# The last LayerNorm's weight and bias are read from PSUM by VectorE

## The reference, cut to what matters

```python
def _layernorm(x, w, b):
    xf = x.astype(jnp.float32)
    mu = jnp.mean(xf, axis=-1, keepdims=True)
    xc = xf - mu
    var = jnp.mean(xc * xc, axis=-1, keepdims=True)
    return (xc * lax.rsqrt(var + LN_EPS) * w.astype(jnp.float32) + b.astype(jnp.float32)).astype(x.dtype)
...
        moe = _hier_moe(h1, ...)
        ple = jax.nn.sigmoid(h1 @ w_ple_gate[i] + b_ple_gate[i]) * (p[i] @ w_ple[i])
        h = _layernorm(DN_ALPHA * h1 + moe + ple, ln2_w[i], ln2_b[i])
```

## Time and profile before

| what | value |
|---|---|
| median of 3 runs | 893.3 us (891.83 to 893.46) |
| the profiled execution's own time | 893.97 us |
| its span, first to last instruction | 892.2 us |
| mean granted TensorE clock | 0.966 |
| busy share of the span: PE, DVE, ACT, POOL | 87%, 49%, 20%, 18% |

### The profile page before, as it was taken

The page is one execution under the profiler, slowest core; times in us unless marked ns, Lnnn a source line. Parts: engine busy times, 40 slices in busy tenths (PEclk is TensorE's granted clock), DMA queues, the critical chain, the costliest instruction groups (busy, mean ns, idle before and its releaser), DMA issues.

```text
span 892.2 us, 9829 instructions
## 1 busy us (share of the span) xinstructions
PE 778.1 (87%) x3913; PEld 527.0 (59%) x3913; DVE 436.9 (49%) x743; ACT 179.4 (20%) x333; POOL 156.1 (18%) x74
## 2 busy tenths in 40 slices
PE   0399997799999999999999999999999989988700
PEld 0388786789887888544444688885554544544200
DVE  5999806455668888311135678362212220211138
ACT  4212323344232321000000110121111111111022
POOL 5734663220042221100000060000000000000042
PEclk9999998899999999999999999999999999999955
DMA  9523321111121132622110351807999999999562
GB/s 294 191 93 96 94 94 48 48 49 48 48 95 48 48 82 61 239 91 79 63 47 1 139 239 47 327 4 279 423 424 422 423 422 421 423 423 422 228 212 95
DMA packets 57860, 163.48 MB, mean 183 GB/s; under 512 B 14412, under 2 KB 37078, under 8 KB 45014
## 3 DMA queue, kind: packets, MB, share of 16 engines
q1 hardware_dynamic: 51744, 139.68, 41.2%
q0 software_dynamic: 3072, 12.63, 4.0%
q10 hardware_dynamic: 2998, 10.53, 2.9%
HBM read 148.15 MB, written 14.68 MB: 182 GB/s over the span
## 4 chain that ended last, share of the span: by engine, by line
PE 71%; DMA 15%; DVE 9%; issue 2%; ACT 1%; POOL 1%; SPq 1%; ACTq 0%; DVEq 0%; POOLq 0%
PE psum L744 24%; DMA ring<-in_w_exp_up_dram 11%; PE psum L1038 9%; PE psum L953 6%; PE psum L943 6%; PE psum L992 5%; PE psum L1053 3%; PE psum L934 3%; PE psum L1015 2%; DMA ring<-in_w_in_dram 2%; PE psum L1016 2%; DVE arena L1398 2%; PE psum L883 2%; DVE arena L1397 2%; PE psum L903 1%
## 5 line engine op out<-in xcount | busy, mean ns | idle before, releaser
L744 PE MATMUL psum<-ring_r 128*128 128x512 f32 (+1 forms) x768 | 213.3, 363 | 2.6 <-DVE arena L1569 1.3
L744 PEld LDWEIGHTS psum<-ring_r 128*128 128x128 f32 x768 | 139.4, 194 | 26.2 <-issue 2.4
L675 POOL TENSOR_TENSOR ring_r<-ring,ring_r 128x2048 fp32r<-128x2048 f32 x20 | 93.4, 4670 | 205.5 <-ACT ring_r L1109 205.5
L1038 PE MATMUL psum<-ring,arena 128*64 128x512 f32 x512 | 113.1, 594 | 11.5 <-DMA ring<-in_w_exp_up_dram 10.7
L1109 ACT COPY arena<-psum 128x512 f32<-128x512 f32 (+3 forms) x102 | 57.5, 582 | 290.8 <-PE psum L960 139.8
L744 PE MATMUL psum<-arena_r,ring_r 128*128 128x512 f32 x256 | 100.5, 392 | 0.0
L1038 PEld LDWEIGHTS psum<-ring,arena 128*64 128x64 f32 x512 | 40.2, 137 | 82.7 <-issue 81.8
L1824 DVE SCALAR_TENSOR_TENSOR arena<-arena,psum 128x256 f32<-128x256 f32 x16 | 9.9, 621 | 120.5 <-ACT arena L1291 120.5
L707 POOL DMA_INDIRECT ring<-y_rows,rowsU x8 | 9.1, 1132 | 328.5 <-ACT arena L1109 326.4
L1015 PE MATMUL psum<-arena_r 128*128 128x256 f32 x256 | 65.3, 293 | 0.0
L1016 PE MATMUL psum<-arena_r 128*128 128x256 f32 x256 | 62.5, 282 | 0.0
(11 more groups left out here) (242 smaller groups left out, 956.8 us busy)
## 6 DMA issues: line engine op xcount, KB each, us to landing
ring<-in_w_exp_gate_dram SPq DMA_DIRECT2D x32, 1024.0 KB, 17.3
ring<-in_w_exp_up_dram SPq DMA_DIRECT2D x32, 1024.0 KB, 19.5
ring<-in_w_exp_down_dram SPq DMA_DIRECT2D x32, 1024.0 KB, 19.4
ring<-in_w_in_dram SPq DMA_DIRECT2D x18, 1024.0 KB, 5.1
y_rows<-arena ACTq DMA_DIRECT2D x16, 512.0 KB, 8.0
y_rows<-arena POOLq DMA_DIRECT2D x4, 1024.0 KB, 7.2
ring<-in_w_out_ssd_dram SPq DMA_DIRECT2D x4, 1024.0 KB, 7.3
ring<-in_w_out_dram SPq DMA_DIRECT2D x4, 1024.0 KB, 11.1
```

The source lines that it names most:

```text
L675: g.tensor_tensor(lo, ring[:, SLOT_OF[seq]], hi.bitcast(F32), ALU.subtract).then_inc(s_w_lo, 1)
L744: t = mm(o, a, b, start=(first and j == 0), stop=(last and j == 2))
L1038: t = mm(psum[sides[half], parity, :], xgT[buf][:, k, c:c + CAP], ring[:, s:s + 2, k, :], start=(k == 0), stop=(k == KD - 1))
```

## The change

PE gets a step behind its overflow loop. It waits for `ln2_in` and then issues four matrix products. Each has as its stationary side one row of 128 ones, and as its moving side 512 columns of row 0 of `A1w` or `A1b`; the product is that piece of the row in all 128 partitions. The weight comes to stand in PSUM banks 0 and 1, the bias in banks 2 and 3, and a new semaphore `pe_ln2` tells that the four are done. DVE waits for `pe_ln2` in the place where it waited for `ln2_in`, and passes the two PSUM views to `tiles_normed`. POOL's tile 3 still reads `A1w` and `A1b` in SBUF. The first LayerNorm is as it was.

```diff
+        s_pe_ln2 = sem("pe_ln2")
...
                     down(j + PAIRS, j + PAIRS // 2, 0)
                 pe.nop()
+            pe.wait_ge(s_ln2_in, 32)
+            for j, row in enumerate((A1w, A1b)):
+                for b in range(2):
+                    t = mm(psum[:, 2 * j + b, :], ones[0:1, :], row[0:1, 512 * b:512 * b + 512], start=True, stop=True)
+            t.then_inc(s_pe_ln2, 1)
...
             dve.wait_ge(s_act_stats, 1 + NT - 1)
-            dve.wait_ge(s_ln2_in, 32)
-            tiles_normed(base, A1w, A1b, s_fin_ready)
+            dve.wait_ge(s_pe_ln2, 1)
+            w2, b2 = (psum[:, 2 * j:2 * j + 2, :].rearrange("p b n -> p (b n)") for j in range(2))
+            tiles_normed(base, w2, b2, s_fin_ready)
```

## The result

| | median us | lowest to highest | runs |
|---|---|---|---|
| kernel before, in this comparison | 892.11 | 891.48 to 893.46 | 5 |
| changed kernel | 888.15 | 886.34 to 888.97 | 5 |

The ratio is 0.9947, with a 95% interval of 0.9931 to 0.9964: the change makes the kernel 0.4 to 0.7% faster. The medians lie 3.96 us apart. The gain of 3.92 us that the forecast rests on agrees with the difference of the medians and lies inside the interval (3.2 to 6.2 us). The profiled execution took 888.41 us, with a span of 886.7.

The account below looks back on a forecast made before the run. The tail was taken as DVE's six norm steps plus 3.1 us, with PE busiest but unaffected. Tile 1's waits gave -3.92 us, other terms 0; from the median 893.3 that made 889.4 us, range 888.2 to 891.5.

Parts of the forecast that it names:

- the base of the sum: Whole kernel: the starting time for the forecast, the median 893.3 us, from which the gain was taken.
- The waits inside tile 1's steps: Final norm, DVE: tile 1's two steps stop waiting for POOL, 3.24 to 1.28 us each, -3.92 us.
- A PSUM input costs nothing: Final norm, DVE's six steps: reading the second input from PSUM adds 0 us.
- The far end: Final norm: PSUM slow as second input, 2.49 us a step, 896.6 us in all; rival's chance 3%.
- The open point, the second input from PSUM instead of the first: Tile 1's norm steps: input order might matter and free nothing, time staying at 893.3 us; rival's chance 7%.
- POOL at 2.2 us a step: Tile 3's norm: POOL's two steps lose their waits, some 2.2 us each, ending about 883.3 instead of 885.36.
- The rival of a POOL that keeps its pace: Tile 3's norm: POOL steps take 3.2 us by themselves, delaying tile 2's store; 890.9 us; chance 8%.
- The store queue: Kernel's end: ACT's stores of tiles 1, 3 and 2 don't hold each other up, 0 us.
- PE's products, 4.8 us, all hidden: Behind PE's overflow loop: four new products take 4.8 us, done by 858.1, and DVE's wait costs 0.
- The cover: Between PE's new products and DVE's wait at 874.93: 16.8 us of slack.

Follow-up runs that it names:

- e1: The changed kernel run once more with no edit: 887.12 us, ratio 0.9940 to the kernel before.
- e5: The changed kernel with POOL's two steps on tile 3 left out: 887.68 us, ratio 0.9953 to the kernel before.
- e8: The changed kernel with only the bias read from PSUM, the weight in SBUF: 889.35 us, ratio 0.9984 to the kernel before.
- e2: The changed kernel with PE's spreading and DVE's wait kept, but weight and bias read in SBUF: 891.45 us, ratio 0.9993.
- e4: The kernel before with POOL's two steps on tile 3 left out: 888.67 us, ratio 0.9963.
- e3: The changed kernel with only the weight read from PSUM, the bias in SBUF: 888.85 us, ratio 0.9966 to the kernel before.
- e6: The changed kernel with the first LayerNorm's weight and bias also spread into PSUM by PE: 884.69 us, ratio 0.9911 to the kernel before.
- e7: e6 with PE spreading the first norm's weight once landed, and separate DVE waits for weight and bias: 881.0 us, ratio 0.9881.

## Why the prediction was wrong, and where it was right

**The step that failed is the base of the sum.** The prediction took -3.92 us from "the median 893.3", a median of three runs, and put the range's lower end 1.2 us under the 889.4 that came of it. In the comparison the kernel before had a median of 892.11 (five runs, the three among them), and in the later ones 892.12, 892.32 and 891.54, over 27, 11 and 17 runs; single runs reach from 887.22 to 896.02. Three runs stood 1.2 us too high. From 892.11 the same sum gives 888.19, and 888.15 was measured. That this agrees to 0.04 us is luck, as is the miss of 0.05 us: the changed kernel's next six runs have a median of 887.12, and all eleven one of 887.38. What the text said of the spread ("889.4 may read a us lower") took the base for certain to about a us, with three runs that already differed by 1.6.

**Where the spread comes from.** The programs of the two kernels and of e1 to e5 and e8 are the same ahead of PE's last product, so their profiles show what changes from execution to execution. The first projection starts between 40.85 and 42.80 us; ahead of it DVE waits for input tiles whose landing varies (its last such wait ends at 12.81 us in the kernel before and at 11.67 in e5). From POOL's L675 at 117.21 (before) to the one at 190.88 it is 73.67 us, in the changed kernel 73.13, in the others 71.12 (e8) to 73.12. From there to the next, at 248.87, it is 57.99 us, with the change 57.99 as well, in e8 58.00; and from the issue of ln2's weight to the first gather it is 342.12 to 342.26 us in all eight. From the first gather to the norm it is 22.33 to 22.93 us, 22.91 before and 22.41 with the change. The stretch that varies most is that of the attention, where PE waits often and its clock falls. Windows of 10 us of the kernel before, with their length, PE's busy time (and rows), granted clock, DMA share and GB/s:

```profile
140.00:150.00 10.00, 5.58 (x50) 0.94 0.21 75
150.00:160.00 10.00, 8.25 (x54) 0.72 0.00 0
```

The same of e8:

```profile
140.00:150.00 10.00, 3.98 (x32) 0.81 0.00 0
150.00:160.00 10.00, 10.00 (x76) 0.85 0.17 49
```

How the clock's falls lie in this stretch differs between executions. That this makes the 2.5 us (73.67 against 71.12) was not tried by itself. The norm's earlier start after the change, 1.6 us, lies within this spread (873.81 to 877.29 in the eight profiles), and e2 shows it with no change of time.

Point by point:

- *The waits inside tile 1's steps, -3.92 us*: right. The tail won 3.94; e4 shows that POOL is the cause, and e3 and e8 that the turns are taken step by step.
- *A PSUM input costs nothing*: right, to 0.02 us over six steps (e4 against e5). The far end, 2.49 us a step, is out. So is the overhead that the Trainium skill states (Perfetto Trace Analysis, section Optimizing Scalar/DVE Operations): by its 60 and 125 ns the steps would have taken some 1.34 us, an estimate from that page, and they took 1.27 and 1.28.
- *The open point, the second input from PSUM instead of the first*: settled by the change itself. The steps read SBUF first and PSUM second and wait for nothing. With this both orders agree with the rule that the Trainium skill states (SBUF — State Buffer, section Who interferes with whom).
- *POOL at 2.2 us a step*: nearly right. The 2.2 us were the exclusive part, 2.21 us in e3 and e8; the whole step takes 2.35. Tile 3 is ready at 881.98, 1.57 us ahead of DVE. The rival of a POOL that keeps its pace is out.
- *The store queue, 0*: right. The end follows DVE's last step by 3.15 us.
- *PE's products, 4.8 us, all hidden*: mis-sized and without effect. They took 6.42 us. Each counts as two rows of PE, and the 594 ns were the length of one row, which overlaps the next; at the lower clock it is 0.86 us from one row to the next. The cover was 16.8 us as said. In e6, where there is no such cover, DVE waited 5.11 us for them.

What stays open: the four kernels whose tails are equally short (the change, e1, e4, e5) gained 4.7, 5.4, 3.3 and 4.2 us by their ratios, 4.4 in the mean, where the tail has 3.9; the medians of the eleven runs of the changed kernel (887.38) and of the 60 of the kernel before (892.1) differ by 4.7. The remainder of 0.5 to 0.8 us is smaller than the width of each interval, and is not explained. PE's part alone, at 0.6 us (between 1.6 faster and 0.4 slower), may hold something or nothing.

## What to carry to other kernels

Look for DVE steps of one shape with two durations: if the longer ones lie beside POOL's steps and read two tensors from SBUF, one of the inputs placed in PSUM sets both engines free. A row that is the same in all partitions can be put there by PE with one row of ones, for nothing where PE is idle and the data have landed, and at the price of a wait where DVE needs the row first (5.11 us in e6, none in e7 after an earlier start). Before a gain of half a percent is set on a base, take that base from more runs than three, and compare stages of the profiles, since the span mixes the gain with the spread ahead of it.

## What the runs showed of the hardware

DVE steps with two SBUF inputs and POOL steps with two SBUF inputs take turns: while 1.08 us of a 1.28 us DVE step run, the POOL step stands, and while 2.21 us of a 2.35 us POOL step run, the DVE step stands (e3, e8). This was exact enough to work out e8's DVE steps to 0.01 us ahead of its run. With one of DVE's inputs in PSUM, first or second (the changed kernel, e3, e8), DVE doesn't wait, and with the second there POOL doesn't either.

PE's fp32 products of 512 columns come as two rows each. With a single row of contraction these start 0.86 us apart at a granted clock of 0.50 (the last six of the change's eight rows, behind 851 us) and 0.43 us apart at 1.00. The latter is seen in e8, where the clock fell only near the end of the products (a row of the timeline, then two windows of 1 us):

```profile
846.51 4.42 PE L1106 MATMUL psum<-arena 1*128 1x512 f32 x8 [2.01 <-issue]
...
847.00:848.00 1.00, 1.00 (x4) 1.00 0.42 168
850.00:851.00 1.00, 0.93 (x2) 0.50 0.00 0
```

A contraction of 128 rows has the same spacing, 55.1 us for 128 rows or 0.43 each, in the kernel before:

```profile
L943 PE MATMUL psum<-arena,ring 128*128 128x512 f32 x128 | 55.1, 592 | 0.0
```

So a small contraction makes the products no cheaper. At the start of e6 and e7 the spacing is 0.86 us as well (7.16 us for eight rows), though the clock's column reads 1.00 there. The profiles have no record of the clock ahead of 39.9 us (e6) and 30.3 us (e7), so the column says nothing of that stretch.
